# A delta-rule mixer whose triangular inverse is built in two 64-row halves, with its decays sent as exact rows and two of its fill units moved

## The reference

```
lower = where(strict, (k*beta) @ k.T * decay, 0)      # per chunk and head
t_inv = (I + lower)^-1                                # unit lower triangular
u = t_inv @ (v*beta);  w = t_inv @ (k*beta*exp(gc))
attn = q @ k.T * decay
for each chunk:                                       # the recurrence, state is 128x128 per head
    v_new = u - w @ state
    o     = (q*exp(gc)) @ state + attn @ v_new
    state = state*exp(g_last) + (k*exp(g_last-gc)).T @ v_new
```

## Time and profile before

| | us |
|---|---|
| median of 3 runs | 2381.65 (2379.84 to 2381.73) |
| the profiled execution, its own time | 2382.03 |
| its span, first to last instruction | 2380.2 |
| mean granted TensorE clock | 0.996 |
| PE busy | 2340.7 (98%) |
| PE weight loads busy | 1917.6 (81%) |
| DVE, ACT, POOL busy | 890.0, 771.4, 1283.1 |

### The profile page before, as it was taken

How to read it: one execution, slowest core, us unless ns; L and a number is a source line. 1 busy time by engine, 2 the same in 40 slices (tenths; PEclk the granted TensorE clock), 3 DMA queues, 4 the chain that set the end, 5 groups by cost and what they waited for, 6 DMA issues and landing times.

```text
span 2380.2 us, 29590 instructions
## 1 busy us (share of the span) xinstructions
PE 2340.7 (98%) x11798; PEld 1917.6 (81%) x11798; DVE 890.0 (37%) x1404; ACT 771.4 (32%) x1537; POOL 1283.1 (54%) x732
## 2 busy tenths in 40 slices
PE   8999999999999999999999999999999999999998
PEld 7798877787877888888887988767778778888887
DVE  3653314343355431123356523243443445211233
ACT  5533325323136231122355442262140353211121
POOL 5511653564553566677655126635555535666774
PEclk9999999999999999999999999999999999999999
DMA  4300331332231333333223013313322313333331
GB/s 152 98 27 28 89 89 53 98 89 72 79 100 44 106 107 97 98 98 98 80 77 89 19 36 91 87 47 113 89 80 71 93 49 95 119 98 97 97 95 66
DMA packets 105753, 196.84 MB, mean 83 GB/s; under 512 B 8464, under 2 KB 18832, under 8 KB 105360
## 3 DMA queue, kind: packets, MB, share of 16 engines
q1 hardware_dynamic: 104464, 188.65, 26.2%
q10 hardware_dynamic: 1152, 6.29, 0.8%
HBM read 192.82 MB, written 2.10 MB: 82 GB/s over the span
## 4 chain that ended last, share of the span: by engine, by line
PE 91%; DVE 5%; ACT 3%; issue 1%; DMA 0%; DVEq 0%; ACTq 0%
PE big L1686 66%; PE mix L1686 9%; PE mix L1824 5%; DVE c_lo L1429 1%; PE big L2000 1%; PE mix L1968 1%; PE mix L1894 1%; PE mix L2069 1%; PE mix L1979 1%; PE mix L1787 1%; PE mix L2201 1%; PE mix L2150 0%; DVE scr L1441 0%; PE mix L1741 0%; PE mix L2134 0%
## 5 line engine op out<-in xcount | busy, mean ns | idle before, releaser
L568 POOL TENSOR_SCALAR ring_hi<-stage 128x1024 fp32r<-128x1024 f32 (+3 forms) x364 | 372.1, 1022 | 1042.6 <-PE big L1686 962.2
L570 POOL TENSOR_TENSOR ring_lo<-stage,ring_hi 128x1024 fp32r<-128x1024 f32 (+3 forms) x364 | 912.6, 2507 | 30.4
L1686 PE MATMUL big<-h_hi,ring_hi 128*128 128x512 f32 (+1 forms) x1888 | 720.3, 382 | 2.8 <-DVE h_lo L1149 1.5
L1686 PE MATMUL big<-h_hi,ring_lo 128*128 128x512 f32 (+1 forms) x1888 | 709.9, 376 | 0.0
L1686 PE MATMUL big<-h_lo,ring_hi 128*128 128x512 f32 (+1 forms) x1888 | 709.9, 376 | 0.0
L1686 PEld LDWEIGHTS big<-h_hi,ring_hi 128*128 128x128 f32 x1888 | 355.7, 188 | 75.3 <-issue 9.0
L1686 PEld LDWEIGHTS big<-h_lo,ring_hi 128*128 128x128 f32 x1888 | 355.6, 188 | 65.4
L1686 PEld LDWEIGHTS big<-h_hi,ring_lo 128*128 128x128 f32 x1888 | 355.8, 188 | 63.8 <-issue 1.9
L1628 DVE TENSOR_TENSOR h_lo<-scr,h_hi 128x1024 fp32r<-128x1024 f32 x64 | 84.7, 1324 | 248.4 <-ACT h_hi L1067 248.4
L1686 PE MATMUL big<-ring_hi,h_hi 128*128 128x512 f32 x448 | 174.5, 391 | 0.0
L1686 PE MATMUL big<-ring_lo,h_hi 128*128 128x512 f32 x448 | 174.3, 391 | 0.0
(11 more groups left out here) (292 smaller groups left out, 2826.3 us busy)
## 6 DMA issues: line engine op xcount, KB each, us to landing
stage<-in_w_in SPq DMA_DIRECT2D x168, 512.0 KB, 3.5
stage<-in_w_mlp_in SPq DMA_DIRECT2D x64, 512.0 KB, 3.6
stage<-in_w_mlp_out SPq DMA_DIRECT2D x64, 512.0 KB, 3.8
stage<-in_w_o SPq DMA_DIRECT2D x16, 512.0 KB, 3.8
stage<-in_w_br_a SPq DMA_DIRECT2D x8, 512.0 KB, 3.8
stage<-in_w_br_c SPq DMA_DIRECT2D x8, 512.0 KB, 3.8
stage<-in_w_br_d SPq DMA_DIRECT2D x8, 512.0 KB, 3.9
stage<-in_w_br_b SPq DMA_DIRECT2D x8, 512.0 KB, 3.5
```

Of the source, the lines that this page charges most:

```text
L568: nc.gpsimd.tensor_scalar(rH[jw][0:pp, r, 0:kk, 0:job.n], w, 1.0, 0.0, ALU.mult, ALU.add).then_inc(sem("w_hi"), 1)
L570: nc.gpsimd.tensor_tensor(rL[jw][0:pp, r, 0:kk, 0:job.n], w, f32(rH[jw][0:pp, r, 0:kk, 0:job.n]), ALU.subtract).then_inc(sem("w_ready"), 1)
L1686: ins_ = MM(o_, a_, r_, start=s0, stop=s1)
```

## The change

It replaces the 128x128 working matrices of the inverse by two 64x64 diagonal blocks, stacked in the two halves of the partitions (`HALVES`): levels 1 to 5 run on these, as 64x64 products in pairs that use rows 0 to 63 into PSUM partitions 0 to 63, and rows 64 to 127 into 64 to 127; only the last level (n = 6) forms the off-diagonal 64x64 block. Transposes become products with the identity. There is one bank per block and step in place of two. `lower` forms the three 64x64 blocks that are needed (12 products for 4). `decays` takes four products of 256 columns of an exact row matrix (`g_rows`, high and low parts) in place of eight float32 ones; it is prepared once in a layer by two small products (`gt`) and four short DVE instructions. The exponents move to ACT (`row_exponents`, nine ACT instructions for a block, where there were three on ACT and three on DVE). DVE and ACT do the lower matrices before the convolutions of the values. Two fill units, split in halves by tiles, stand ahead of `T0` in place of three, and blocks 0 and 1 of the recurrence have their one fill in two halves; block 2 has two fills in place of one. Outside the delta rule, one copy of a gate tile on ACT is issued earlier (`gate_c_copy`), and the last 512 KB store is cut in two.

```diff
             def decays(b):
-                per_head_tile(("R", b), lambda o_, h: MM1(o_, s_g[:, b, h:h + 1].to_broadcast((P, P)), triu))
-                per_head_tile(("B", b), lambda o_, h: MM1(o_, s_be[:, b, h:h + 1].to_broadcast((P, P)), ident))
+                mix_freed(pe, "gt")
+                for name, row in (("R", 8), ("B", 0)):
+                    ps = tile_of((name, b))
+                    for q in range(2):
+                        at = CROW - CRD + row + 2 * b + q
+                        i = MM1(ps[:, 2 * P * q:2 * P * (q + 1)], rot_r[:, at:at + 1].to_broadcast((P, P)), g_rows[:, :])
+                    done(i, (name, b))
...
             def lower(b):
...
-                per_head_tile(("LT", b), lambda o_, h: MM1(o_, tokens(aK, h, b), g_kb[b % 2][:, h, :]))
+                ps, near = tile_of(("LT", b)), slice(0, HB)
+                for h in range(GH):
+                    k, kb = tokens(aK, h, b), g_kb[b % 2][:, h, :]
+                    for rows in HALVES:
+                        MM1(ps[rows, h * HB:(h + 1) * HB], k[:, rows], kb[:, rows])
+                    i = MM1(ps[near, (GH + h) * HB:(GH + h + 1) * HB], k[:, near], kb[:, HB:P])
+                done(i, ("LT", b))
...
-            do("av", between=value_unit)
-            set_fill("gatea0", "az")
-            fill(1)
+            for i in range(2):
+                unit(JOB["av"], i)
+                value_unit(i)
+            unit(JOB["av"], 2, (0, 1))
+            value_unit(2)
+            unit(JOB["av"], 2, (2, 3))
+            decays(0)
+            decays(1)
+            unit(JOB["av"], 3, (0, 1))
             for i in range(4, 8):
                 mix_freed(pe, ("l2", i))
-            for b in range(2):
-                if b:
-                    decays(b)
-                    fill(1)
-                lower(b)
-                scores_gdn(b)
-            fill(1)
-            pe.wait_ge(*upto("a_silu", 12))
+            lower(0)
+            scores_gdn(0)
+            unit(JOB["av"], 3, (2, 3))
+            lower(1)
+            scores_gdn(1)
+            set_fill("gatea0", "az")
+            for tiles in ((0, 1), (2, 3)):
+                for q in range(2):
+                    unit(*fills[q], tiles)
+            del fills[0:2]
...
+                        for h in range(GH):
+                            if n < LEVELS - 1:
+                                for rows in HALVES:
+                                    i = MM1(ps[rows, h * HB // 2:(h + 1) * HB // 2], blocks(g_LTm[e])[rows, h, :],
+                                            level_half(blocks(g_T[e])[rows, h, :], n, 0))
+                            else:
+                                i = MM1(ps[HB:P, h * HB:(h + 1) * HB], blocks(g_LTq[e])[:, h, :], blocks(g_T[e])[0:HB, h, :])
+                        done(i, key)
...
+                                for rows in HALVES:
+                                    at = slice(h * HB // 2, (h + 1) * HB // 2)
+                                    i = MM1(ps[rows, at], blocks(g_V[e])[rows, h, :], g_Yc[e][rows, at])
...
+                                i = MM1(ps[0:HB, h * HB:(h + 1) * HB], blocks(g_Yq[e])[:, h, :], g_U[e][HB:P, h, HB:P])
+                        done(i, key)
...
+                            for rows in HALVES:
+                                one = ident[rows, rows] if n == LEVELS - 2 else level_half(ident[rows, rows], n, 1)
+                                w = HB if n == LEVELS - 2 else HB // 2
+                                i = MM1(ps[rows, h * w:(h + 1) * w], blocks(g_T[e])[rows, h, :], one)
+                        done(i, key)
...
+                    natural_k_v(b)
...
                     if ahead:
                         decays(b + 2)
-                    fill(1)
-                    mix_freed(pe, ("ks", b))
...
-                    per_head_tile(("new", b), lambda o_, h: MM1(o_, g_U(e, h), g_vb[:, h, :]))
+                    if b < NT - 2:
+                        half_unit(0)
+                    else:
+                        fill(1)
                     if ahead:
                         lower(b + 2)
-                    elif b == NT - 1:
+                    mix_freed(pe, ("ks", b))
+                    mix_freed(pe, ("X", b, LEVELS - 1))
+                    per_head_tile(("new", b), lambda o_, h: MM1(o_, g_U[e][:, h, :], g_vb[:, h, :]))
+                    if b < NT - 2:
+                        half_unit(1)
+                    else:
                         fill(1)
...
+            def row_exponents(b):
...
+                for h in range(GH):
+                    A(g_dec[e][:, h, :], R[:, h, :], ACT.Relu, bias=s_gc[:, b, h:h + 1], scale=-1.0).then_inc(sem("a_arg"), 1)
...
+                mix_free(A(eR_of(b), R, ACT.Exp), ("R", b))
...
+                for rows in HALVES:
+                    A(blocks(g_decc[e])[rows], g_dec[e][rows, :, rows], ACT.Exp, scale=-1.0).then_inc(sem("a_decc"), 1)
+                A(s_ed[:, b, :], g_dec[e][:, :, P - 1], ACT.Exp, scale=-1.0).then_inc(sem("a_ed"), 1)
...
+                A(g_dec[e], g_dec[e], ACT.Exp, scale=-1.0).then_inc(sem("a_dec"), 1)
...
+            for b in range(2):
+                beta_keys(b)
+            for b in range(2):
+                lower(b)
+                scores_out(b)
+                first_level(b)
             for i in range(8, 12):
                 conv(i)
+            row_decays(0)
```

More of the change, by code:

```diff
@@ L39 @@
 SBH = 8
+HB = 64
 DIL = (1, 4, 4)
@@ L92, in shape_constants @@
     levels = []
-    for n in range(7):
-        z = 1 << n
-        levels.append(one((c // (2 * z) == p // (2 * z)) & (c % (2 * z) >= z) & (p % (2 * z) < z)))
+    for n in range(6):
+        z, q, r = 1 << n, p % HB, np.arange(HB)[None, :]
+        levels.append(one((r // (2 * z) == q // (2 * z)) & (r % (2 * z) >= z) & (q % (2 * z) < z)))
     k = np.arange(2 * P)[None, :]
@@ L663, in gate_copy, with gate_c_copy @@
                     big_free(A(gate_at(b, hf)[:, i, :], ps[:, :], ACT.Copy), (f"gate{b}{hf}", i))
-            def gate_c_copy(q):
+            def gate_c_copy(q, tiles=range(2)):
                 if q == 0:
                     big_freed(act, ("ya1", 3))
-                for i in range(2):
+                for i in tiles:
                     ps = big_wait(act, (f"gatec{q}", i))
@@ L1219, in level_mask, with level @@
                 e = b % 2
-                if n > 1:
-                    for c in range(2):
-                        mix_wait(dve, ("Y", b, n - 1, c))
-                TT(g_LTm[e], g_LT[e], per_mask(consts[:, CLV + n * P:CLV + (n + 1) * P]), ALU.mult).then_inc(sem(f"a_LTm{e}"), 1)
+                mix_wait(dve, ("Y", b, n - 1))
+                TT(blocks(g_LTm[e]), blocks(g_LT[e]), level(n), ALU.mult).then_inc(sem(f"a_LTm{e}"), 1)
             def per_mask(ap):
                 return ap.unsqueeze(1).to_broadcast((P, GH, P))
+            def level(n, rows=slice(0, P)):
+                return consts[rows, CLV + n * HB:CLV + (n + 1) * HB].unsqueeze(1).to_broadcast((rows.stop - rows.start, GH, HB))
             if l == 0:
@@ L1400, in vector_layer @@
                     scores_out(3)
-                    row_decays(3)
             def head_normed(h, o, rs, tag):
@@ L1714, in half_fill, with half_unit @@
                 unit(*(fills[0] if t == 0 else fills.pop(0)), (t,))
+            def half_unit(t):
+                unit(*(fills.pop(0) if t else fills[0]), (2 * t, 2 * t + 1))
             def set_fill(*names):
@@ L2155, in value_step @@
                     done(r, ("wpv", i))
-            def half_unit(t):
-                unit(*(fills.pop(0) if t else fills[0]), (2 * t, 2 * t + 1))
             for p in range(PAIRS + 1):
@@ L2255, in _ @@
                 x_out = out.rearrange("a (t p) d -> p (a t) d", p=P)
-                for t in range(NT):
+                for t in range(NT - 1):
                     for hf in range(2):
@@ L2259, in _ @@
                     sp.dma_start(x_out[:, t, :], xv[:, t, :]).then_inc(stored, 16)
-                sp.wait_ge(stored, 16 * NT)
+                for hf in range(2):
+                    cs = slice(hf * 512, hf * 512 + 512)
+                    big_freed(sp, (f"dn{hf}", NT - 1))
+                    sp.dma_start(x_out[:, NT - 1, cs], xv[:, NT - 1, cs]).then_inc(stored, 16)
+                sp.wait_ge(stored, 16 * (NT + 1))
             @block.gpsimd
```

312 lines of the change are left out of this document (161 added, 151 removed), and 10 rows, old and new, of the table PER_LAYER.

## The result

The changed kernel takes 2396.8 us (median of 4 runs, 2394.9 to 2400.0) against 2381.0 for the one before on the same chip: ratio 1.0069, 95% interval 1.0056 to 1.0081. It is slower, by 16 us. The forecast was 2352. The time is that of the first rival, "the clock falls in the levels" (2395), and lies outside the forecast's own range; but the trace shows that the clock is not the whole cause.

What follows compares the result with a forecast made beforehand. PE's line of instructions was taken to bound the kernel, busy 98% of the span. Terms 4.9 - 0.3 + 8.8 + 3.0 - 0.8 - 1.0 + 0.3 gave 14.9 us per layer, 30.1 in all: about 2352, range 2340 to 2396.

Steps and rivals of the forecast that it cites:

- The forecast: Whole kernel: about 2352 us, with granted clock 1.00 from T0 to ks; chance 45%, its own range 2340 to 2362.
- first rival: Levels: PE's granted clock falls to half, 43 us lost over four pairs, 2395; chance 26%.
- today's wait ahead of `o`: PE's wait for the copy ahead of o: among today's waits of 3.1 us per layer, each said to lose its cause.
- The earlier gate copy: End of the kernel: a gate copy issued earlier saves 0 to 0.5 us, taken as 0.
- `lower(3)`: Block 1: PE waits 1.0 us per layer, as DVE needs about 6.7 and PE has 5.9 of work.
- a rival (2.2 per layer): Other waits: DVE's products wait for POOL, 2.88 in place of 0.69; part of the 2362 to 2380 rival, chance 14%.
- The wait behind `T0`: Between T0 and block 0's first Y: PE waits 1.8 us per layer for DVE and ACT work.
- Decays: Four 256-column matmuls per block, 0.12 apart, 0.48 us in place of 1.71; 4.9 us per layer saved.
- second rival: Levels: the two row halves don't overlap in one bank, 56 ns a record, 39 us lost, 2391; chance 12%.
- The step: Levels: 1.20 us per step, set by latency, so 3.6 per level in place of 4.48; 8.8 per layer saved.
- The last level: Y and X, 16 records each at 56 ns, way round 0.3: 2.1 us in place of 3.6; 3.0 per layer saved.
- new waits: At T0 and lower(3): 1.8 and 1.0 us per layer, against 3.1 of today's waits; net 0.3 saved.

Runs made afterwards that it cites:

- e2: Changed kernel with three units ahead of the first transposes, as before the change, and one in place of two in block 2: 2364.3 us, ratio 0.9937.
- e10: Kernel with the third unit back ahead of the first transposes, plus eight DVE writes of zeros making PE wait in the second pair's levels: 2377.1 us, against 2364.3 without.
- e14: Kernel with the third unit ahead and row_decays(2) late, plus one whole unit ahead of Y of level 4 in the second pair only: 2358.7 us.
- e7: Kernel before the change with only the units' place changed, the third moved from ahead of T0 to block 2: 2390.2 us, ratio 1.0050.
- e1: Changed kernel with ACT's copy of the gate's bank moved from behind block 0's o copy to behind block 1's: 2384.7 us, ratio 1.0014.
- e12: Changed kernel with ACT's table load moved behind the copies of T0 in the first pair of blocks: 2385.4 us, ratio 1.0025.
- e17: Changed kernel with the banks of its last four keys named 0, 1, 2, 3 in place of 1, 2, 3, 0: 2390.0 us, ratio 1.0041.
- e15: Changed kernel with three units ahead of T0, two tiles ahead of Y of levels 3 and 5, row_decays(2) late, gate's copy inside the levels: 2348.5 us.
- e18: Fastest version (two tiles twice in the levels, three units ahead, row_decays(2) late; 2348.5) with its last four keys' banks named 0, 1, 2, 3: 2340.6 us.
- e3: Changed kernel with one spare 128-row, 256-column matmul at the head of each T0, Y, X and V bank: 2498.8 us, ratio 1.0502.
- e6: Kernel with the third unit ahead of the first transposes (2364), with row_decays(2) also late on DVE: 2361.0 us, ratio 0.9919.
- e16: Changed kernel with gate's copy behind block 1's o copy, table load behind the first T0 copies, row_decays(2) late, no unit moved: 2367.9 us, ratio 0.9936.
- e4: Changed kernel with two spare 128-row, 256-column matmuls at the head of each T0, Y, X and V bank: 2444.0 us, ratio 1.0268.
- e5: Changed kernel with one tile ahead of Y of levels 1 to 4 of each pair, two units ahead of T0, one unit per block: 2374.2 us, ratio 0.9966.

## Why the prediction was wrong

**The step that failed** is the choice between the forecast (granted clock 1.00 from `T0` to `ks`, 45%) and the first rival (26%). I gave the clock's fall the smaller chance, having seen that the levels lay between a stretch that kept it and one that lost it. The runs showed that the levels can run at 1.00 (12 us in the first pair of e2, 15 in its second) but don't hold it. A gap can tip them: behind 2.94 both second pairs of e10 fell, and behind 1.63 both first pairs of the changed kernel. They can also fall without one (e14). Once down they stay down, in e14 for 27 us with PE busy, where the old work is back at 1.00 after 3.4 us (e7). Price: at 1.00 a level takes 3.13 and at 0.50 5.12, so that 1 us at 0.50 loses 0.39. Executions of one kernel agree: those of e10 go from 2368.9 at 0.985 to 2383.9 at 0.978, 15 us for 0.007 x 2 x 2376 = 33 us at 0.50, or 0.45 us for each; those of e1 and e12, taken likewise, give 0.44 and 0.34. The changed kernel has 106 us more of it than the one before: some 42 us of loss, 36 to 48. The rival had 43. It took all four pairs as down for most of their levels; the first pairs were down for nearly all of theirs, the second layer's second pair for 17 us of 25, and the first layer's for the last 8 of 21. That its 2395 is so near 2397 is partly luck: waits that it did not have came on top, and a better step than it assumed came off.

**The wait I took as gone.** The prediction has today's wait ahead of `o` among those that lose their cause, as "a half or whole unit lies ahead of each `o`". It is 5.5 in each layer, 11 us (e1). The sum looked at how much work PE has there, not at what ACT has to wait for. ("The earlier gate copy" of the prediction is `gate_c_copy`, another instruction; the one that waits is `gate_copy("a", 0)`, which stayed in its place and has no term.) A step that is moved also moves whoever waits for it: I listed what queued behind `lower(3)` on PE, and not which of ACT's instructions wait for a fill.

**The wait that I sized too small.** `lower(3)`: 1.0 forecast, 3.3 measured. I had seen DVE's product slowed beside POOL (2.88 against 0.69) and put it into a rival (2.2 per layer) in place of the sum; with it the sum would have been 3.2.

**The one I didn't look for.** 249 small-bank keys per layer in place of 316: the change removes 67, and the remainder by four puts the next layer's first key on the bank that is freed last. 4.1 us, and 6.8 with its time at 0.50 (e17). The count could have been made from the order of keys.

**What was right.** The wait behind `T0`: 1.8 forecast, 1.63 measured. Decays: four records, 0.12 apart, as the earlier trace rows. The two halves run side by side, so that the second rival is refuted: 33 ns a record in one bank. By the Trainium skill (TensorEngine Tiling (Array Packing), Restrictions and Gotchas) they could not use the same bank at once; at other partitions of it they do here, and the measurement decides. The step was better than I took: 1.04 and not 1.20, so a level of 3.13 and not 3.6, 9.4 us more gain in both layers. The last level was worse. In e15, with the clock at 1.00, its last `V` records, `Y` and `X` are these:

```profile
199.78 0.97 PE L1881 MATMUL mix<-consts,scr 64*64 64x64 f32 x26
...
202.43 1.11 PE L1881 MATMUL mix<-scr 64*64 64x64 f32 x16 [0.75 <-issue]
203.47 0.66 PE L1907 MATMUL mix<-consts,scr 128*128 128x128 f32 x4
```

From the end of `V` (about 200.8) to `kn` at 203.47 it is 2.7 and not 2.1: the way round over ACT costs 0.75, not 0.3, 2.4 us in all.

**The sum again.** My 2352, less 9.4 for the levels, plus 2.4 for the last one, plus 11.1 at `o(1)`, 4.6 at `lower(3)`, 4.1 at the boundary: 2365. With 42 for the clock it is 2407, where 2397 was measured; the 10 between them were not taken apart. For e18, whose clock is as that of the kernel before, the sum comes near: 2352, less 9.4, plus 2.4, less the 5.6 of new waits that were in it, plus 3.0 for the 1.5 at each `o(1)`, is 2342; measured 2340.6. It leaves out 1.5 us of pauses in two steps and, as an estimate from e3's rows, some 2 us for the changes of form at eight places in the levels, so that some 5 us of gain have no term.

**What stays open.** What tips the clock: behind 0.20 and 0.84 it fell in the first layer of the kernel with the table load late, and in its second the levels ran on at 1.00 for 14 us more; in e14 it fell with no gap. And why PE pauses in the middle of a step with no semaphore. In two kernels with the same instructions on PE the pause comes at the same record (here e6; e2 above):

```profile
132.46 1.12 PE L1863 MATMUL mix<-scr,g_uc 64*64 64x32 f32 x31 [0.38 <-issue]
```

so it seems to go by the place in PE's stream. In e10 the same step takes 0.3 longer than its neighbours, and in e14, at 0.50, it has no pause. The delivery of instructions would fit (two per 33 ns); no run here shows it.

## What to carry to other kernels

When a change makes PE's work thinner, the time saved is only had if the clock stays; put work that PE must do anyway, in pieces of some 3 us, into the thin stretch rather than behind it. Taking out the gaps alone was not enough here (e16, and the first pair of e14). Before a filler is moved, list every engine's instruction that waits for its result or for the buffer that it frees, and count the uses of rotating banks again. The same arithmetic was 0.7% slower or 1.7% faster than the kernel before by order alone.

## What the runs showed of the hardware

- The granted clock has a memory that depends on the work: behind a gap of 2.8 us PE's 128-row work was back at 1.00 after 3.4 us (e7); behind a gap of 2.9 us the 64-row levels, with PE busy for all of the time, stayed at 0.50 for 17 us (e10). In e14 they fell with no gap ahead and stayed down for 27 us, through the whole of the levels and into the work behind them. The Trainium skill (TensorE: Matmul & The Clock Gate, A second HAM failure mode: psum-queue depth-cycling) tells of short idle times between groups of matmuls that make the clock swing; these traces agree in part: the clock fell behind gaps of 0.24 to 2.9 us, but it did not swing in the levels, it stayed down, and PE need not be idle for it to fall or to stay down.
- Mixing one dense matmul into every 16 thin records made it worse (clock 0.952, e3), two held it in three pairs of four (0.981, e4). Each change of form costs PE about 0.13 us (a bank of e3 grew by 0.37 with one matmul of 0.11 and two changes) to 0.2 (0.32 between starts in place of 0.12).
- DVE's products of two SBUF operands stand still while POOL's split runs: 2.84 in place of 0.68. The Trainium skill (SBUF — State Buffer, SBUF: two separate sides) says that the two share a port pair as an exclusive lock; the trace agrees. So the first matmul behind a unit, which gives its slot back and starts the split, is itself an event to place (e5).
- A PSUM bank was written by both row halves of the array at once, on different partitions, at 33 ns a record (changed kernel, 187.69 to 197.00).
